# Deeper rings of split weights (high 6 to 7, low 5 to 7) and both engines six halves ahead, in an fp32 three-block network on one core

## Time and profile before

| | us |
|---|---|
| median of 3 runs (lowest, highest) | 974.69 (974.21, 975.08) |
| span of the profiled execution | 973.0 |
| PE busy | 964.8 (99%) |
| PE weight load busy | 825.9 (85%) |
| DVE busy | 701.5 (72%) |
| ACT busy | 551.6 (57%) |
| POOL busy | 154.1 (16%) |

### The profile page before, as it was taken

The page is one execution under the profiler, slowest core; times in us unless marked ns, Lnnn a source line. Parts: engine busy times, 40 slices in busy tenths (PEclk is TensorE's granted clock), DMA queues, the critical chain, the costliest instruction groups (busy, mean ns, idle before and its releaser), DMA issues.

```text
span 973.0 us, 14065 instructions
## 1 busy us (share of the span) xinstructions
PE 964.8 (99%) x5352; PEld 825.9 (85%) x5352; DVE 701.5 (72%) x1085; ACT 551.6 (57%) x949; POOL 154.1 (16%) x189
## 2 busy tenths in 40 slices
PE   9999999999999999999999999999999999999997
PEld 8878888888888888888888888888888888988885
DVE  6888676766666757786667656666758989778884
ACT  6688665444555554455456444554535857766662
POOL 2741018920001102220001000000550110000000
PEclk9999999999999999999999999999999999999999
DMA  9985545565554664345555665555544463643631
GB/s 340 297 225 192 181 130 183 194 222 181 173 195 154 216 214 131 130 134 212 173 173 179 202 209 189 173 186 179 208 153 153 151 196 111 193 132 130 216 131 43
DMA packets 110339, 174.73 MB, mean 180 GB/s; under 512 B 4289, under 2 KB 73025, under 8 KB 110273
## 3 DMA queue, kind: packets, MB, share of 16 engines
q1 hardware_dynamic: 109840, 173.40, 54.3%
q10 hardware_dynamic: 432, 0.44, 0.1%
HBM read 172.78 MB, written 1.05 MB: 179 GB/s over the span
## 4 chain that ended last, share of the span: by engine, by line
PE 92%; DVE 3%; POOL 1%; issue 1%; DMA 1%; SPq 1%; ACT 0%; POOLq 0%; DVEq 0%
PE ps L552 24%; PE ps L505 19%; PE ps L503 11%; PE ps L445 9%; PE ps L447 9%; PE ps L446 9%; PE ps L502 3%; PE ps L521 2%; PE ps L680 1%; PE ps L660 1%; PE ps L519 1%; PE ps L648 1%; DMA xs<-in_x 1%; PE ps L604 1%; DVE wlo L1536 1%
## 5 line engine op out<-in xcount | busy, mean ns | idle before, releaser
L1536 DVE TENSOR_TENSOR wlo<-raw,whi 128x1024 fp32r<-128x1024 f32 x312 | 373.3, 1235 | 16.4 <-PE ps L552 8.3
L1027 ACT ACTIVATE whi<-raw 128x1024 fp32r<-128x1024 f32 x312 | 315.5, 1048 | 35.6 <-PE ps L552 21.8
L505 PE MATMUL ps<-hT,whi 128*128 128x512 f32 x784 | 279.5, 396 | 0.0
L503 PE MATMUL ps<-hT,wlo 128*128 128x256 f32 x896 | 231.7, 279 | 0.0
L552 PE MATMUL ps<-whi,ur 128*128 128x512 f32 x656 | 181.6, 389 | 0.0
L503 PEld LDWEIGHTS ps<-hT,wlo 128*128 128x128 f32 x896 | 168.9, 188 | 9.1
L505 PEld LDWEIGHTS ps<-hT,whi 128*128 128x128 f32 x784 | 147.1, 188 | 30.3
L552 PEld LDWEIGHTS ps<-whi,ur 128*128 128x128 f32 x656 | 123.0, 188 | 24.4
L445 PE MATMUL ps<-whi,hT 128*128 128x512 f32 (+1 forms) x312 | 122.1, 391 | 0.0
L447 PE MATMUL ps<-whi,hT 128*128 128x512 f32 (+1 forms) x312 | 120.0, 385 | 0.0
L446 PE MATMUL ps<-wlo,hT 128*128 128x512 f32 (+1 forms) x312 | 119.9, 384 | 0.0
(11 more groups left out here) (233 smaller groups left out, 1310.6 us busy)
## 6 DMA issues: line engine op xcount, KB each, us to landing
raw<-in_w SPq DMA_DIRECT2D x64, 1024.0 KB, 5.6
raw<-in_w_in SPq DMA_DIRECT2D x34, 1024.0 KB, 5.1
raw<-in_w_in_o SPq DMA_DIRECT2D x24, 1024.0 KB, 5.2
raw<-in_w_out_o SPq DMA_DIRECT2D x8, 1024.0 KB, 4.9
raw<-in_w_in_e SPq DMA_DIRECT2D x5, 1024.0 KB, 13.1
raw<-in_w_mem SPq DMA_DIRECT2D x4, 1024.0 KB, 12.1
raw<-in_w_out_e SPq DMA_DIRECT2D x4, 1024.0 KB, 5.1
raw<-in_w_out SPq DMA_DIRECT2D x4, 1024.0 KB, 4.9
```

Of the source, the lines that this page charges most:

```text
L503: mm = e.matmul(o[:, 0:256], l[:, k, :], hT[0][:, k, :], start=False, stop=False)
L505: mm = e.matmul(o, h[:, k, :], both, start=False, stop=k == 7)
L1027: e.activation(split_half(i)[0], raw_half(i), ACT.Copy).then_inc(*up("hi", ("hi", i)))
L1536: e.tensor_tensor(l, raw_half(i), h.bitcast(F32), ALU.subtract).then_inc(*up("lo", ("lo", i)))
```

## The change

The low ring grows from five to seven halves and the high ring from six to seven, and both engines work six halves ahead. The 12 KB a partition for this come out of the space reserved for descriptors of dynamic DMAs, cut to 1024 bytes; nothing in the program uses it. HI_ROW, LO_ROW, all orders and all instructions stay as they are.

```diff
-NRAW, NHI, NLO = 4, 6, 5
-HI_AHEAD, LO_AHEAD = 5, 4
+NRAW, NHI, NLO = 4, 7, 7
+HI_AHEAD, LO_AHEAD = 6, 6
...
-    nc = bacc.Bacc("TRN2", target_bir_lowering=False, num_devices=1)
+    nc = bacc.Bacc("TRN2", target_bir_lowering=False, num_devices=1, dynamic_dma_scratch_size=1024)
```

## The result

The changed kernel takes 992.07 us (990.13 to 993.46, four runs) against 974.85 us of the kernel before on the same chip (974.21 to 975.08): a ratio of 1.0176, 95% interval 1.0161 to 1.0190. A second set of five runs took 991.83 us (990.55 to 993.44), ratio 1.0174 (1.0160 to 1.0188). It is slower, as forecast, by 17.2 us where 12.5 were forecast; 992.07 stands 0.07 above the upper end of the range. The profiled span is 989.9 us, 16.9 more than before, and the median lies 2.2 us above it, not 1.7. Three of the ten executions of the kernel with M, D and X opened, further down, took 1373.8, 1613.2 and 2491.4 us beside seven of 976.2 to 976.9; they are left out of its median and ratio.

The account below looks back on a forecast made before the run. PE was taken as the bound, busy 964.8 of 973.0 us. Start 1.4, M 2.4, D 0 and X 8.7 sum to 12.5: span 985.5, with 1.7 for the median 987.2 us; 8-in-10 range 975.6 to 992.

Parts of the forecast that it names:

- M: Branch M: DVE's splits wait for ACT's high parts, rope comes late and PE stalls 2.4 us; bounds 0 and 4.8.
- D: Branch D: lags of 2 to 5 us arise, but DVE waits for PE anyway; taken as 0.
- X: Branch X: waiting for ACT's high part closes a loop of ACT and DVE; +8.7 us, bounds 2 and 11.
- What bounds it; ring waits: Whole kernel: PE never stands for a weight half, so deeper rings can gain at most 0.5 us.
- Start: Kernel start: extra early splits delay `ka`; PE stands 1.9 us, the wait near 64 us goes, net +1.4.
- The bound of 2.9 us: Kernel start: upper bound of the cost, the whole delay of ACT's squares of `ka`.
- D's bound of 1 us: Branch D: upper bound of a cost taken as 0, with some tenths of slack at PE's last product of values.
- the loop: Branch X: ACT's and DVE's work in one chain over two steps, 9.05 us a unit against PE's 6.7.
- The last step: Branch X, step 8: DVE's low part of unit 3's transposes, needed by `x_values(1)`, comes later: +1.7 us.
- the entry: Branch X, first unit: probabilities come at 867.05 instead of 865.15, two locks, 1.9 us.
- only PE's pace counts: Rival, whole kernel: added waits are covered, only the 0.5 us wait goes, 974.2; 0.15 together with the last rival.
- start alone: Rival: waits in branches M and X are hidden, only late `ka` costs, 976.1 us; chance 0.12.

Follow-up runs that it names:

- M, D and X opened: Changed kernel, but DVE's lead is five, ACT's six, from branch M's first gate label to the end: 976.62 us, ratio 1.0018.
- the rings alone: Changed kernel with rings of seven and seven halves, but the old leads of 5 (ACT) and 4 (DVE): 974.75 us, ratio 1.0001.
- (6, 5): Changed kernel with ACT's lead 6 and DVE's 5, so ACT is again one call ahead: 974.71 us, ratio 0.9999.
- X opened: Changed kernel, but DVE's lead is 5 from the calls of Xg on: 981.86 us, ratio 1.0069.
- D opened: Changed kernel, but DVE's lead is 5 from Dg to just before Xg: 989.67 us, ratio 1.0148.
- the run at 976.0: Changed kernel, both leads six through qa, ka, qb and kb, DVE's five from then on: 976.00 us, ratio 1.0014.
- (5, 5): Changed kernel with both leads 5, so ACT as far ahead as before and DVE one half more: 990.56 us, ratio 1.0164.
- X filled: Changed kernel, but PE computes the gate product before its longest wait in branch X twice: 992.58 us, ratio 1.0178.

## Why the prediction was right in its kind and short in its size

**What bounds it; ring waits.** Right. No wait for a half arose or went, and the rings alone are worth nothing (ratio 1.0001).

**Start.** The chain is right, and its sum came out near by some luck. Forecast: squares of `ka` at 29.9, sums at 31.7, second block done at 38.05, net 1.4. After, everything runs 0.6 to 0.7 us earlier from the first loads on. ACT's, DVE's, POOL's and PE's rows:

```profile
29.03 0.42 ACT L1045 ACTIVATE arena<-ps 128x128 f32<-128x128 f32 x2
```

```profile
31.21 0.47 DVE L1560 TENSOR_REDUCE stat<-arena 128x2 f32<-128x128 f32 x2
31.60 2.35 DVE L1536 TENSOR_TENSOR wlo<-raw,whi 128x1024 fp32r<-128x1024 f32 x2
...
37.22 0.34 DVE L1579 TENSOR_SCALAR arena<-ps,stat 128x128 f32<-128x128 f32 x1
```

```profile
31.58 2.42 POOL L2262 TENSOR_SCALAR stat<-stat 128x2 f32<-128x2 f32 x1 [1.01 <-DVE stat L1560]
...
35.30 0.27 POOL L2262 TENSOR_SCALAR stat<-stat 128x2 f32<-128x2 f32 x1
```

```profile
37.45 0.41 PE L616 MATMUL ps<-cst,arena 128*128 128x128 f32 x2 [1.08 <-DVE arena L1577]
```

PE takes the second block at 37.45, 1.25 us later than before, and 1.3 us is what the start alone costs by the medians. Counted from where the trace stands at 20 us, PE loses 2.0 us up to there and 1.8 stay (forecast 1.9 and 1.4), since the wait near 64 us, which was to go, only shrank from 0.5 to 0.25 us. The early loads hide 0.7 of that in this trace; the second trace of the changed kernel has no such head start. POOL's first step took 2.42 us again behind two DVE splits and its second 0.27, as the term assumed. The Trainium skill (SBUF — State Buffer, two separate sides) has a POOL operation that reads SBUF and a DVE operation with two SBUF inputs shut each other out, the later one for the whole of the other; the rows agree, and no run here put the first of POOL's two steps where no DVE split runs. The bound of 2.9 us took ACT's late squares for the cost, and the leads (6, 5) show that they cost nothing by themselves.

**M: the mis-sized term.** The mechanism held and its first number was close (a wait of 4.42 us, forecast 4.7). The split that was to begin at 740.5 plus what the start had already cost, 1.4, begins at 741.88:

```profile
741.88 1.23 DVE L1536 TENSOR_TENSOR wlo<-raw,whi 128x1024 fp32r<-128x1024 f32 x1 [4.42 <-ACT whi L1027]
...
766.34 1.23 DVE L1536 TENSOR_TENSOR wlo<-raw,whi 128x1024 fp32r<-128x1024 f32 x1 [1.56 <-ACT whi L1027]
...
770.30 0.87 DVE L1801 SCALAR_TENSOR_TENSOR arena<-ps,stat,cst 128x256 f32<-128x256 f32 x2
```

```profile
769.13 0.44 PE L660 MATMUL ps<-cst,arena 128*128 128x128 f32 x2 [1.21 <-DVE arena L1801]
771.23 0.44 PE L660 MATMUL ps<-cst,arena 128*128 128x128 f32 x2 [1.66 <-DVE arena L1801]
```

The second lock is 1.56 us (forecast 1.6). DVE gives back less than I had allowed: with PE's own lateness of 1.4 taken off, rope's end is 3.85 us late, not 3.3, and PE loses 3.2 us in two waits, not 2.4 in one. Then the clock: 1.6 us in the matmuls behind the waits. The prediction named a change of the granted clock as something not reckoned with, and that is the larger half of M's miss: 4.8 us by the slips and by opening it, against 2.4. The size of this term is partly chance: the trace with X opened, the same in M, has no fall, and the one with D opened a longer one.

**D: "I take 0" failed.** I asked only whether PE stands in D. It does not (0.2 us), but DVE leaves D 2.2 us late instead of the few tenths with which I let it enter X. D's bound of 1 us was wrong for the same reason.

**X: the loop was right.** Scaling of the probabilities (L1119) in ACT's timeline:

```profile
874.33 0.91 ACT L1119 ACTIVATE arena<-arena,stat 128x256 f32<-128x256 f32 x2 [1.37 <-DVE stat L1700]
...
882.16 0.91 ACT L1119 ACTIVATE arena<-arena,stat 128x256 f32<-128x256 f32 x2 [1.37 <-DVE stat L1700]
...
891.10 0.91 ACT L1119 ACTIVATE arena<-arena,stat 128x256 f32<-128x256 f32 x2 [1.37 <-DVE stat L1700]
...
900.82 0.91 ACT L1119 ACTIVATE arena<-arena,stat 128x256 f32<-128x256 f32 x2 [1.54 <-DVE stat L1700]
```

Intervals 7.83, 8.94 and 9.72 us; forecast 7.8, 9.0 and 9.85. The last step cost PE 1.4 to 1.5 us (forecast 1.7), and PE's 4.1 us for the bank of `gate_added` were foreseen as 4. What is off is the entry: unit 0's probabilities are done 3.7 us late beyond PE, forecast 1.9. That is D's 1.8. Slow matmuls of PE lie beside this chain and cost nothing.

**The account.** Forecast 12.5 on the span, measured 16.9: 1.7 in X through D, 0.8 for the waits of M, 1.6 for the clock, 0.3 near 305 us, 0.2 in D, 0.4 at the start, less 0.7 by which this trace was ahead from the first loads; 0.1 I can't place. The rest of the difference of 4.9 us between 987.2 and 992.07 is the offset of median and span, 2.2 where the kernel before had 1.7. Of the rivals, "only PE's pace counts" fell with the loop's 9 us a unit, and "start alone" has its own price in the run at 976.0. So the steps that failed are two terms of the sum: M, put at 2.4 us and worth 4.8, and D, put at 0 and worth 2.4, of which 2.2 fall due in X.

## What to carry to other kernels

When two engines make the two parts of one product and the second part needs the first, the difference of their leads can be the resource, as it is here, and not the depth of either: (5, 4) and (6, 5) run alike, (5, 5) and (6, 6) lose 16 to 17 us, although no consumer ever waited for a part. Count the lock where the second engine also serves a chain that the bounding engine waits for; 32 us of such waits over the stages up to the second MLP cost 0.4, 28 us over the branches cost 15. And carry each engine's lateness across stage borders even where the bounding engine doesn't stand: the stage that pays can be the next.

## What the runs showed of the hardware

- PE's granted clock fell to 1.2 GHz behind stands of 1.2 and 1.7 us close together, behind one of 4.1 us, and in the kernel with X filled behind one of 2.65 us, in kernels where PE is busy 98% of the time; a fall made the matmuls behind it lag by 1.5 or 1.6 us, a longer one in M (0.50 instead of 0.72 over the same 6 us) by 2.6. With the stands of M filled by work done twice the clock stayed up there (1.00 over 769 to 777 us) and the kernel was 2.0 us faster for 2.7 us more matmuls.
- The same stands of 1.2 and 1.7 us went without a fall in one trace. Standing is thus not the whole condition. Of four runs of one program, D opened, one has a mean granted clock of 0.999 and three 0.993 to 0.996.
- A fall that lies behind another engine's chain costs nothing: PE reached 901.87 with it and 901.88 without.
- With the space reserved for descriptors of dynamic DMAs cut to 1024 bytes and 12 KB a partition of it given to tiles, the time of this program didn't change: 974.75 against 974.69 us.
